# Hyena layer: another order of the output projection's pieces and of their weight granules

## What is computed

```python
def attn_conv_mixer(h, w_in, q_gain, k_gain, sinks, conv_w, w_out):
    q, k, v, gate_b, gate_c, u = jnp.split(h @ w_in, EVEN_SPLITS, axis=-1)
    ...
    attn = sliding_window_attention(q, k, v, sinks)
    conv = gate_b * causal_depthwise_conv(gate_c * u, conv_w)
    return jnp.concatenate([attn, conv], axis=-1) @ w_out
```

## Time and profile before

| | |
|---|---|
| median of 3 runs | 2094.9 us |
| the profiled execution | 2091.03 us |
| its span, first to last instruction | 2089.2 us |
| mean granted TensorE clock | 0.98 |
| busy: PE | 1965.7 us, 94% |
| busy: DVE | 1569.6 us, 75% |
| busy: ACT | 1237.0 us, 59% |
| chain that ended last: PE, DVE, ACT | 84%, 8%, 4% |
| layer h's attention steps, scores of item 0 to the ffn's first matmul | 665.1 to 734.2 us |

### The profile page before, as it was taken

One profiled execution on the slowest core, in us unless ns is written; L12 is line 12 of the kernel. 1 busy time (PEld: TensorE's weight loads), 2 busy tenths in 40 slices (PEclk: granted clock), 3 DMA queues, 4 the chain that ended last, 5 costly groups with the idle time before them and its releaser, 6 DMA issues.

```text
span 2089.2 us, 26476 instructions
## 1 busy us (share of the span) xinstructions
PE 1965.7 (94%) x9460; PEld 1641.2 (79%) x9460; DVE 1569.6 (75%) x1873; ACT 1237.0 (59%) x1448; POOL 143.2 (7%) x209
## 2 busy tenths in 40 slices
PE   7988989899969899998989999999999999999998
PEld 6766867677759688886878878888888888888886
DVE  6663985857556554445868888888989888898986
ACT  5461134755644453443757767777777777777775
POOL 3113401313001000000000000000000000000000
PEclk9999999999989999999999999999999999999999
DMA  8422333324324255553339979898998989989894
GB/s 321 152 81 78 104 131 136 121 90 173 121 81 142 81 201 184 191 189 123 159 126 377 373 307 370 335 375 338 366 376 331 374 339 367 371 333 375 331 374 175
DMA packets 70518, 499.99 MB, mean 239 GB/s; under 512 B 8736, under 2 KB 8736, under 8 KB 10528
## 3 DMA queue, kind: packets, MB, share of 16 engines
q1 hardware_dynamic: 70432, 498.87, 63.6%
HBM read 497.79 MB, written 1.05 MB: 239 GB/s over the span
## 4 chain that ended last, share of the span: by engine, by line
PE 84%; DVE 8%; ACT 4%; issue 3%; POOL 1%; DMA 0%; DVEq 0%; SPq 0%; ACTq 0%; POOLq 0%
PE psum L987 24%; PE psum L989 23%; PE psum L988 23%; PE psum L1820 4%; DVE low L954 3%; ACT high L951 2%; PE psum L3183 2%; PE psum L3244 1%; PE psum L1828 1%; PE psum L1231 1%; ACT h L1554 1%; POOL small L1215 0%; DVE x L1322 0%; PE psum L1450 0%; PE psum L1836 0%
## 5 line engine op out<-in xcount | busy, mean ns | idle before, releaser
L954 DVE TENSOR_TENSOR low<-raw,high 128x2048 fp32r<-128x2048 f32 (+1 forms) x460 | 1047.0, 2281 | 296.6 <-ACT high L951 295.5
L951 ACT ACTIVATE high<-raw 128x2048 fp32r<-128x2048 f32 (+1 forms) x460 | 877.3, 1911 | 401.3 <-PE psum L989 383.0
L987 PE MATMUL psum<-high,yT_high 128*128 128x512 f32 (+1 forms) x1672 | 666.4, 399 | 40.1 <-issue 13.6
L989 PE MATMUL psum<-high,yT_low 128*128 128x512 f32 (+1 forms) x1672 | 655.8, 392 | 0.0
L988 PE MATMUL psum<-low,yT_high 128*128 128x512 f32 (+1 forms) x1672 | 654.8, 392 | 0.0
L987 PEld LDWEIGHTS psum<-high,yT_high 128*128 128x128 f32 x1672 | 317.1, 190 | 111.3 <-issue 31.5
L989 PEld LDWEIGHTS psum<-high,yT_low 128*128 128x128 f32 x1672 | 316.9, 190 | 67.7
L988 PEld LDWEIGHTS psum<-low,yT_high 128*128 128x128 f32 x1672 | 317.7, 190 | 61.6
L987 PE MATMUL psum<-high,hT_high 128*128 128x512 f32 (+2 forms) x560 | 220.9, 394 | 11.2 <-DVE h L1731 6.1
L989 PE MATMUL psum<-high,hT_low 128*128 128x512 f32 (+2 forms) x560 | 217.3, 388 | 0.0
L988 PE MATMUL psum<-low,hT_high 128*128 128x512 f32 (+2 forms) x560 | 217.0, 388 | 0.0
(11 more groups left out here) (347 smaller groups left out, 1732.6 us busy)
## 6 DMA issues: line engine op xcount, KB each, us to landing
raw<-in_moe_weights SPq DMA_DIRECT2D x336, 1024.0 KB, 4.8
raw<-in_weights SPq DMA_DIRECT2D x132, 1024.0 KB, 4.9
raw<-in_weights SPq DMA_DIRECT2D x2, 896.0 KB, 4.7
raw<-in_weights SPq DMA_DIRECT2D x2, 768.0 KB, 7.9
x<-in_x SPq DMA_DIRECT2D x2, 512.0 KB, 4.0
raw<-in_weights SPq DMA_DIRECT2D x2, 512.0 KB, 3.7
out_x<-x SPq DMA_DIRECT2D x1, 1024.0 KB, 6.1
const<-in_constants SPq DMA_DIRECT2D x1, 512.0 KB, 8.0
```

The source lines that it names most:

```text
L951: eng.activation(high, raw, ACT.Copy).then_inc(k.high_ready, 1)
L954: eng.tensor_tensor(low, raw, high.bitcast(F32), ALU.subtract).then_inc(k.low_ready, 1)
L987: pe.matmul(out, lhs.high, rhs.high, start=start, stop=False)
L989: return pe.matmul(out, lhs.low, rhs.high, start=False, stop=stop)
```

## The change

`H_OUT_ORDER`, the order of the output granules, becomes (0, 1), (0, 0), (1, 1), (1, 0), and the array that is packed on the host follows it. In `H_BESIDE` the pieces at steps 12 and 17 change places. Nothing else is edited; bank numbers, ticks, due steps and the places of the splits in ACT's and DVE's programs are derived from these two.

```diff
-H_OUT_ORDER = [(0, 1), (1, 1), (0, 0), (1, 0)]
+H_OUT_ORDER = [(0, 1), (0, 0), (1, 1), (1, 0)]
@@
-    10: [("piece", (0, 1, 0))], 12: [("piece", (1, 1, 0))], 15: [("piece", (0, 0, 0))], 17: [("piece", (0, 1, 1))],
+    10: [("piece", (0, 1, 0))], 12: [("piece", (0, 1, 1))], 15: [("piece", (0, 0, 0))], 17: [("piece", (1, 1, 0))],
     19: [("piece", (1, 0, 0))], H_STEPS - 1: [("piece", (1, 1, 1)), ("piece", (0, 0, 1))],
```

## The result

The changed kernel takes 2096.51 us (median of 20 runs, 2088.85 to 2099.57), the kernel before 2093.32 us (20 runs, 2090.66 to 2095.86). The ratio is 1.0016, with a 95% interval of 1.0009 to 1.0023: about 3 us slower, and inside the 0.2% that the prediction called "within". The two profiled executions differ by 3.83 us (2094.86 against 2091.03).

The account below looks back on a forecast made before the run. The prediction took TensorE (PE) to bound the kernel. Its terms, -3.55 - 0.94 + 5.2 + 2.0 = +2.7 us, on the three-run median of 2094.9 gave 2097.6 us, range 2092.5 to 2100.5.

Follow-up runs that it names:

- add_first_again: Second run: the kernel before with only the step swap, granule (1,0) split behind step 16, output 1's add ahead of the first ffn low split; ratio 0.9971.

## What to carry to other kernels

When work is reordered to free a buffer earlier, list every later user of the same ring of buffers: here the slot that came free earlier was worth 3.9 us in the trace, and another that changed its user cost 6.2, at the start of the next layer. Look at where the refill stands in each engine's queue, not only when its slot comes free. Where a wait ahead of dense matmuls can't be removed, cheap work for PE in it can save the slow stretch behind it: at the gap of 5.17 us it did, in the trace and in the time; at the stall of 3.58 us only one trace shows it.

## What the runs showed of the hardware

**The same gap has no fixed price.** In the first layer, which no edit touches, PE waits 3.08 us for a split (kernel before) or 3.07 us (add_first_again). PE timelines, of the kernel before and then of add_first_again:

```profile
169.14 0.47 PE L987 MATMUL psum<-high,yT_high 128*128 128x512 f32 x1 [3.08 <-DVE low L954]
...
169.91 0.39 PE L987 MATMUL psum<-high,yT_high 128*128 128x512 f32 x1
...
170.62 0.63 PE L987 MATMUL psum<-high,yT_high 128*128 128x512 f32 x1
...
171.90 0.63 PE L987 MATMUL psum<-high,yT_high 128*128 128x512 f32 x1
```

```profile
170.22 0.47 PE L987 MATMUL psum<-high,yT_high 128*128 128x512 f32 x1 [3.07 <-DVE low L954]
...
170.99 0.40 PE L987 MATMUL psum<-high,yT_high 128*128 128x512 f32 x1
...
171.68 0.40 PE L987 MATMUL psum<-high,yT_high 128*128 128x512 f32 x1
```

The first one falls to the slow pace (1.28 us from one L987 to the next instead of 0.69), the second doesn't. Over the 14 profiled executions the 12 matmuls behind this gap took 2.81 to 2.84 us in nine and 4.04 to 5.26 in five. Another split wait of the same length, near 609 us, was followed by full rate (2.81 to 2.84 us) in just those five and by 4.06 to 4.16 us in the other nine. So whether a gap of 3.07 us costs nothing or 2.4 us isn't told by its length. The gap of 4.70 us near 964 was followed by 4.16 to 5.26 us in all 14. Such differences pile up: the piece at step 12 of layer `h` started anywhere from 700.18 to 706.35 us in the 14 profiled executions, with the same work ahead of it. That is twice the effect of this change, so two profiles can be compared only between landmarks around the edit.

**Cheap transposes hold the clock.** With 44 or 30 transposes of 128 by 128 in the waits of 5.2 and 3.6 us, the clock read 1.00 through the wait and the 12 matmuls behind it, in one profiled execution each. I hadn't been sure that such light matmuls would do.
